# Hybrid decoder layer on one core: alternating pieces of the gated unit, w_out block by block, and two recurrent convolutions in front of the centring

## What is computed

```
hm = rmsnorm(x) * (1 + sc1) + sh1
u, gate, conf_a, conf_b, bg_lru, bg_conf = split(hm @ w_in + b_in)
xc    = causal_dwconv(u, width 4)                     # recurrent branch
hseq  = rg_lru(xc)
out_a = (hseq * gelu(gate)) @ w_lru_o
glu   = conf_a * sigmoid(conf_b)                      # the gated unit
dc    = causal_dwconv(glu, width 31)                  # conformer branch
out_b = silu(layernorm(dc)) @ w_conf_o
merged = sigmoid(bg_lru) * out_a + sigmoid(bg_conf) * out_b
x  = x + gt1 * (merged @ w_out)
hf = rmsnorm(x) * (1 + sc2) + sh2
x  = x + gt2 * moe(hf)                                # 16 experts, top 2 of one group
y  = rmsnorm(x)
```

## Time and profile before

| what | us |
|---|---|
| median of three runs | 941.98 |
| the three runs | 941.9, 941.98, 947.51 |
| the profiled execution | 938.98 |
| its span, first to last instruction | 937.2 |
| PE busy in the span | 865.9 (92%) |
| DVE busy | 708.8 (76%) |
| ACT busy | 414.7 (44%) |
| POOL busy | 299.3 (32%) |

### The profile page before, as it was taken

The page is one execution under the profiler, slowest core; times in us unless marked ns, Lnnn a source line. Parts: engine busy times, 40 slices in busy tenths (PEclk is TensorE's granted clock), DMA queues, the critical chain, the costliest instruction groups (busy, mean ns, idle before and its releaser), DMA issues.

```text
span 937.2 us, 13282 instructions
## 1 busy us (share of the span) xinstructions
PE 865.9 (92%) x5477; PEld 727.1 (78%) x5477; DVE 708.8 (76%) x943; ACT 414.7 (44%) x379; POOL 299.3 (32%) x177
## 2 busy tenths in 40 slices
PE   3899999989999999989999996899999999999983
PEld 3798888989988797889994556778887878777851
DVE  3529999999795996992013567789899988988847
ACT  5443232323246223251211123477677777777623
POOL 5344555736520110143310332113232444332010
PEclk9999999999999999999999996899999999999987
DMA  9988668412120140342446114689999999999932
GB/s 317 341 232 288 228 235 286 132 47 91 45 90 2 45 135 1 101 140 91 163 148 258 46 45 186 203 320 348 350 374 340 350 344 362 365 347 346 346 113 96
DMA packets 76538, 194.41 MB, mean 207 GB/s; under 512 B 7972, under 2 KB 49060, under 8 KB 66093
## 3 DMA queue, kind: packets, MB, share of 16 engines
q1 hardware_dynamic: 71245, 182.19, 54.8%
q0 software_dynamic: 5088, 10.99, 4.4%
q10 hardware_dynamic: 144, 0.38, 0.1%
HBM read 185.41 MB, written 16.47 MB: 215 GB/s over the span
## 4 chain that ended last, share of the span: by engine, by line
PE 42%; DVE 33%; DMA 12%; ACT 5%; issue 4%; SPq 2%; POOL 1%; POOLq 0%; DVEq 0%; ACTq 0%
PE ps L1284 16%; DVE ps L1685 13%; PE ps L1272 6%; DVE slot_c L1853 6%; PE ps L1372 6%; DMA ring_a<-in_w_up 5%; PE ps L1466 5%; DMA ring_a<-in_w_gate 4%; PE ps L1489 2%; DVE slot_a L1853 2%; SPq L538 2%; ACT slot_c L1080 2%; PE ps L1316 1%; DVE region_d L1743 1%; DMA region_b<-in_w_ada 1%
## 5 line engine op out<-in xcount | busy, mean ns | idle before, releaser
L756 POOL TENSOR_TENSOR w_lo<-ring_a,w_hi 128x2048 fp32r<-128x2048 f32 x28 | 132.0, 4716 | 251.3 <-ACT w_hi L941 251.3
L1853 DVE TENSOR_TENSOR slot_c<-ring_a,slot_c 128x2048 fp32r<-128x2048 f32 x72 | 164.0, 2288 | 22.5 <-ACT slot_c L1080 22.1
L1284 PE MATMUL ps<-hm_hi,w_hi 128*128 128x272 f32 x720 | 151.8, 292 | 7.7 <-ACT region_c L980 4.0
L1080 ACT ACTIVATE slot_c<-ring_a 128x2048 fp32r<-128x2048 f32 x72 | 137.2, 1916 | 46.3 <-DMA ring_a<-in_w_gate 26.4
L1284 PE MATMUL ps<-hm_lo,w_hi 128*128 128x272 f32 x720 | 148.6, 288 | 0.0
L1284 PE MATMUL ps<-hm_hi,w_lo 128*128 128x272 f32 x720 | 148.6, 289 | 0.0
L1685 DVE SCALAR_TENSOR_TENSOR ps<-region_b,rt,ps 128x512 f32<-128x512 f32 x208 | 137.6, 744 | 0.0
L1284 PEld LDWEIGHTS ps<-hm_hi,w_hi 128*128 128x128 f32 x720 | 112.4, 189 | 22.9 <-issue 18.6
L1466 PE MATMUL ps<-slot_c,xgt_hi 128*128 128x512 f32 x384 | 126.8, 400 | 1.3 <-DVE slot_c L1853 1.3
L1284 PEld LDWEIGHTS ps<-hm_lo,w_hi 128*128 128x128 f32 x720 | 113.2, 189 | 0.0
L1284 PEld LDWEIGHTS ps<-hm_hi,w_lo 128*128 128x128 f32 x720 | 112.8, 190 | 0.0
(11 more groups left out here) (333 smaller groups left out, 1444.4 us busy)
## 6 DMA issues: line engine op xcount, KB each, us to landing
ring_a<-in_w_gate SPq DMA_DIRECT2D x32, 1024.0 KB, 7.9
ring_a<-in_w_up SPq DMA_DIRECT2D x32, 1024.0 KB, 8.5
ring_a<-in_w_down SPq DMA_DIRECT2D x32, 1024.0 KB, 7.3
ring_a<-in_w_in SPq DMA_DIRECT2D x24, 1024.0 KB, 7.1
region_c<-in_w_ada SPq DMA_DIRECT2D x20, 1024.0 KB, 5.6
ring_a<-in_w_conf_o SPq DMA_DIRECT2D x4, 1024.0 KB, 6.3
ring_a<-in_w_lru_o SPq DMA_DIRECT2D x4, 1024.0 KB, 5.1
region_d<-in_w_ada SPq DMA_DIRECT2D x3, 1024.0 KB, 12.9
```

The source lines that it names most:

```text
L756: g.tensor_tensor(w_lo[:, q % 2], raw[split_at[q] % 2], w_hi[:, q % 2].bitcast(F32), ALU.subtract)\
L1080: s_.activation(hi_slot(n), raw_slot(n), ACT.Copy).then_inc(unit_hi, 1)
L1284: ins = mm(ps[:, bank(n) + h, 0:HALF], w[:, q % 2, k, m * P:(m + 1) * P], x[:, k, h * HALF:(h + 1) * HALF], start=(k == 0 and w is w_hi an ...
L1853: v.tensor_tensor(lo_slot(n), raw_slot(n), hi_slot(n).bitcast(F32), ALU.subtract).then_inc(unit_lo, 1)
```

## The change

Three things are done. The stream and the work of the gated unit alternate by pieces: two blocks of conf_a, the same two of conf_b, the next two of conf_a, and so on; POOL's list and `taps_after` are rearranged with it, and the two `mod_finish` steps come one block later. `w_out` of the first tile is written apart: it runs the first seven merged blocks of both output halves as each is ready, waits for the last drain only then, and ends with the eighth block. And the convolutions `lru_conv(0)` and `lru_conv(1)` stand in front of DVE's wait for the mean, together with the wait for `mod_store`.

```diff
 def weight_stream():
-    s = [("in", g) for g in (G_CA, G_CB, G_CA + 1, G_CB + 1, G_U, G_U + 1, G_GATE, G_GATE + 1)]
+    glu = [("in", g + h, c) for h in range(2) for c in range(2) for g in (G_CA, G_CB)]
+    s = [("in", g) for g in (G_U, G_U + 1, G_GATE, G_GATE + 1)]
...
-    return [(kind, g, c) for kind, g in s for c in range(2)]
+    return glu + [(kind, g, c) for kind, g in s for c in range(2)]
...
-        work = []
-        for g in (G_CA, G_CB, G_CA + 1, G_CB + 1, G_U, G_U + 1, G_GATE, G_GATE + 1):
+        work = [("in", g, m) for _, g, c in stream[0:8] for m in (2 * c, 2 * c + 1)]
+        for g in (G_U, G_U + 1, G_GATE, G_GATE + 1):
...
             g.memset(glu[:, :, 0:W30], 0.0).then_inc(conv_new, 1)
+            gate_glu(0)
             split_lo(2)
+            gate_glu(1)
             split_lo(3)
             pool.wait_ge(states_in, 16)
-            gate_glu(0)
             products(0)
-            gate_glu(1)
             split_lo(4)
             gate_glu(2)
+            gate_glu(3)
             split_lo(5)
-            gate_glu(3)
             products(1)
             split_lo(6)
             products(2)
+            gate_glu(4)
+            gate_glu(5)
             split_lo(7)
-            gate_glu(4)
+            products(3)
             split_lo(8)
-            gate_glu(5)
-            products(3)
             gate_glu(6)
+            gate_glu(7)
             split_lo(9)
-            gate_glu(7)
...
-            taps_after = {6: 1, 8: 2, 10: 3, 13: 4, 17: 5, 20: 6, 22: 7}
+            taps_after = {4: 1, 7: 2, 10: 3, 13: 4, 16: 5, 19: 6, 23: 7}
...
-            drained(pe, len(work) - 1)
             drained(pe, len(work) - 2)
-            pe.wait_ge(merged_ok, KC)
+            assert bank(len(work) - 2) == 0
...
+            def w_out_first():
+                for h in range(2):
+                    pe.wait_ge(wo_full[h], 16)
+                    for k in range(KC - 1):
+                        pe.wait_ge(merged_ok, k + 1)
+                        mm(ps[:, h, :], merged[:, k, 0:P], wo[h][:, k, :], start=(k == 0), stop=False)
+                drained(pe, len(work) - 1)
+                pe.wait_ge(merged_ok, KC)
+                for h in range(2):
+                    mm(ps[:, h, :], merged[:, KC - 1, 0:P], wo[h][:, KC - 1, :], start=False, stop=True).then_inc(out_ps, 1)
+
             def w_out(t):
+                if t == 0:
+                    w_out_first()
+                    return
...
                 conformer(k)
-                if k in (1, 4):
+                if k in (2, 5):
                     mod_finish(1 + k // 4)
+            dve.wait_ge(mod_store, 16 * 8)
+            for k in range(2):
+                lru_conv(k)
             n = place[("mean", 0, 0)]
             dve.wait_ge(pair_act, sum(by_act[:n + 1]))
...
             last_rows(0, 62, 0)
-            dve.wait_ge(mod_store, 16 * 8)
-            for k in range(GC):
+            for k in range(2, GC):
                 lru_conv(k)
```

## The result

The changed kernel takes 950.66 us in the median of 20 runs (945.09 to 956.37), the kernel before 941.94 in the median of 20 (937.39 to 947.51): ratio 1.0088, with a 95% interval of 1.007 to 1.0106, so 6.6 to 10.0 us slower. The profiled execution took 950.83, its span is 949.0.

A forecast was written before the change was run, and what follows sets the result against it. DVE was taken as the limit up to 208 us, PE from 209.75. Centring +11.95, clock +1.7 and w_out -1.78 gave +11.9: 950.9 us profiled, 953.9 median, range 938 to 959.

The forecast's parts named there:

- First block: DVE's first convolution block: gate product 10.8 us earlier, but two POOL splits leave 1.2; PSUM run starts near 71.6.
- Later blocks: DVE's later convolution blocks: fifth to seventh end with POOL splits at 184.2, 208.1, 232.0; eighth at 255.0, 4.15 later.
- Two convolutions in front: DVE before the centring: 7.44 us of convolutions take turns with POOL's addition and two splits; centring ends 277.8, 11.95 late.
- The clock: PE idles about 8 us before "var" and restarts at a slow clock: +1.7 us charged once, bounds 0 and 3.4.
- PE's pace: PE's items: wait for ACT and its slow clock go; item 27 drains at 224.7 against 229.48, 4.8 us early.
- w_out: Start of w_out on PE: the last drain and addition no longer hold it, saving 1.78 us, bounds 0 to 1.8.
- that PE sets the centring: Rival at the centring: splits do not hold DVE, eighth block closes by about 238; -6.6, 935.4 us; chance 0.12.
- the lock-step would not come: Rival at the later blocks: splits miss block ends, eighth closes at 250.85; convolutions still cost; 948 to 950; chance 0.20.
- Piece 14: Rival: its load lands 5 us late behind a later store, split 15 hits the eighth block; +4.6, 958.5; chance 0.08.
- That w_out gives nothing: Rival at w_out: DVE, not PE, leads there; +1.8 us on any case; no separate chance, inside the other ranges.
- the closing op could slip past: The 128x32 op closing a DVE block might, read strictly, run beside a split; the sum is the same either way.

The follow-up runs named there:

- Experiment 6: Changed kernel with only POOL's list rearranged, so that splits run while DVE's convolution reads PSUM: median 939.45 us, ratio 0.9958 to the kernel before.
- Experiment 5: Changed kernel, but POOL does the last split (17) only after both centring ops: median 947.26 us, ratio 1.003 to the kernel before.
- experiment 3: Kernel before with only the two recurrent convolutions moved in front of the centring: median 951.62 us, ratio 1.0118 to the kernel before.
- experiment 4: Changed kernel with the two convolutions put back behind the centring, leaving pieces and w_out edits: median 941.94 us, ratio 1.0006 to the kernel before.
- experiment 7: Changed kernel with POOL's splits behind the products and the two convolutions back behind the centring: median 931.0 us, ratio 0.9865 to the kernel before.
- experiment 8: Changed kernel with rearranged splits, convolutions back behind the centring, and split 17 after both centring ops: median 929.57 us, ratio 0.9859 to the kernel before.
- experiment 1: Kernel before with the w_out edit alone: median 938.0 us, ratio 0.9963 to the kernel before.
- experiment 2: Kernel before with the alternating pieces alone, including POOL's list, taps_after and mod_finish: median 947.2 us, ratio 1.0053 to the kernel before.

## Why the prediction was right

The direction, the range and the mechanism held. The range, 938 to 959, was wide enough to hold no change as well (942); what the forecast risked is the direction and the steps below. The median was forecast at 953.9 and is 950.66. The profiled execution was forecast at 950.9 and took 950.83, and that closeness is luck, for executions of this kernel spread from 945.09 to 956.37 and three misses cancel in the profile: the centring is 0.5 less late than said, w_out gives 2.5 instead of 1.78, and 1.1 is lost between "var" and w_out, where the forecast had nothing (the last section has the place). Step by step:

- *First block.* Said: two splits take the gate product's gain, the run starts at 71.6. It starts at 70.19: the second multiply-add over SBUF came through before POOL's products, in 0.75. Of 10.8 us 2.6 are left instead of 1.2. Experiment 6, which starts the run at 64.71 by the order of POOL's list alone, shows that 5.5 of the 8.2 lost are POOL's doing.
- *Later blocks.* Said: the ends of the fifth to seventh block fall into a split and come with its end, 184, 208 and 232. They came at 185.45, 209.37 and 233.26, 0.04 behind the splits' ends. Missed: split 6 caught the end of the second block (4.01 instead of a gate product's 1.15). The eighth closed at 255.70 (said: 255.0), but the miss seems to have helped. Split 11 came 1.4 later than said, at 180.82. Without the 3.77 that split 6 cost, the fifth block's closing op, which began at 181.25, would have begun near 177.5, an estimate from these rows alone, and would have been over before that split. So the blocks fell into step as forecast, but that they did so at the fifth is in part luck; no run takes split 6 alone out of the way.
- *Two convolutions in front.* Said: 7.44 of their own work plus POOL's addition and two splits, centring done at 277.8. They ran from 255.61 to 272.51, 16.9 us, and the centring ended at 277.26. Experiment 5 takes one split out, and 4.4 come back; experiments 3, 4 and 7 give the edit's cost as 11.1, 7.7 and 8.4.
- *The clock.* Said: +1.7 once, on "var". 9.34 - 7.62 = 1.72. In the mean PE ran slowly as well (2.15 for its four matmuls, 1.08 in experiment 8), but the mean is not on the path of this kernel: DVE is in the convolutions until 272.51.
- *PE's pace.* Said: item 27 drained at 224.7; it was drained at 226.01, 3.5 before that of the kernel before. PE then waited 7.70 for the last addition, as expected of an engine that is not the limit.
- *w_out.* Said: -1.78, with bounds of 0 and 1.8. This term of the sum was mis-sized: the pause is gone as told, but its removal is worth 2.1 to 2.7 by the profiles, 3.7 to 4.2 where the clock falls behind the pause. The price came from the earlier trace rows, the row of a profile in which the clock did not fall at that place. This may also account for the 3.2 by which the median was forecast too high. The profiled execution of before, 3.0 below its median, kept the clock there and at the place of the last section too, and its offset was carried over to a kernel in which the first of the two no longer exists. That fits the numbers; no run tests it by itself.

The rivals: that PE sets the centring fell for this kernel (the splits stretch DVE's ops), though experiments 7 and 8 come near it, once the splits are moved: PE goes from its items into the mean there without a pause, at 246.25 and 246.02. That the lock-step would not come fell with the three ends named above. Piece 14 was not late for POOL: ACT waited 2.23 for it, from 217.00 on, but its split ran from 219.00 to 223.64, between block ends. That w_out gives nothing is refuted by experiment 1.

The rule of the Trainium skill (SBUF — State Buffer, "Who interferes with whom") that a DVE op with two SBUF inputs and a GpSimd op that reads SBUF exclude each other for a whole instruction agrees with all these rows. For an op of one input the section names contention in a two-port mode alone, and it lists tensor_scalar among the ops that can enter one and tensor_reduce, on this chip, as one that cannot. The prediction read from it that the closing op could slip past. But that op is a tensor_scalar, and the rows agree with the list: it stood for 4.01 and 4.20, while the tensor_reduce ran through a split in 1.18. That the tensor_scalar was in such a mode is not shown by any row.

## What to carry to other kernels

Before a long POOL op is placed, or DVE work moved, mark which DVE ops have two inputs in SBUF, and which are tensor_scalar ops from SBUF to SBUF: beside POOL they wait here for its whole op, and the wait shows as DVE's busy time or as "issue", not as a wait for POOL. An op with an operand in PSUM, or the tensor_reduce, was not held. Put POOL's long ops beside DVE's runs with an operand in PSUM; here the order of POOL's list alone was worth 12 us at the eighth block, while filling DVE's idle time cost 8 to 11, because POOL lived in that gap. And a pause of PE on the path can cost more than its length, since the matmuls behind it may start at the lower clock (8.80 instead of 7.11 in experiment 2).

## What was not expected of the hardware

The clock after a short pause is not the same in every profile. The ten profiles, one of each kernel, show it at one place: PE is busy at a granted clock of 1.00 in all of them, then pauses 2.65 to 2.67 us before the first item that uses the gated states, in every kernel alike. The first 3.8 us after that pause by windows, in the kernel before:

```profile
419.47:423.27 3.80, 3.80 (x30) 3.80 (x31) 1.92 (x1) 2.32 (x2) 1.41 (x1) 1.00 0.00 0
```

In the changed kernel:

```profile
432.53:436.33 3.80, 3.80 (x20) 3.80 (x21) 1.92 (x1) 2.31 (x2) 1.41 (x1) 0.62 0.00 0
```

The granted clock is 1.00 here in the kernel before and in experiments 7 and 8, and 0.55 to 0.70 in the seven others, with 18 to 22 matmuls in that time instead of 30; the levels are 1.00 (2.4 GHz) and 0.50 (1.2 GHz), so these are stretches with a part at each. From the end of "var" to the end of the items the three profiles at 1.00 take 214.4 to 214.7, the seven others 215.7 to 216.2. The pause of 1.78 before w_out cost the clock in experiment 2 and not before or in experiment 3; behind 3.16 (experiment 5), 3.96, 5.88, 5.92 and 7.51 it was low. The Trainium skill (TensorE: Matmul & The Clock Gate, "Part 1: The HAM clock gate") says that the gate's window of activity runs freely and is not reset when a kernel starts; by that the same pause could be met by a low clock in one execution and not in another. The rows do not contradict it, but no run here shows it: each kernel has one profile, and none shifts a pause in time on purpose.

The stage of the experts also varies between profiles: from its first rows to the end of the span it is 345.6 us before, 345.7 in the changed kernel, 351.4 in experiment 1 and 353.6 in experiment 2, whose profiled executions are 6.6 and 7.4 above their medians; the kernel of experiment 1 runs the same code there as the kernel before. A difference of single profiles says little here until it is split into the part ahead of that stage and the rest.
